# Four seven-product pairs instead of three in each feed-forward layer, the last one split by row blocks at the layer's end

## The reference, cut to what matters

```
D_MODEL, D_FF, SEQ = 1024, 2816, 256

def swiglu(x, w_in, w_out):
    gate, up = jnp.split(x @ w_in, 2, axis=-1)
    return (jax.nn.silu(gate) * up) @ w_out

h = layer_norm(DN_ALPHA * h + 0.5 * swiglu(h, ffn_w_in[i, 0], ffn_w_out[i, 0]), ...)
```

## Time and profile before

| | |
|---|---|
| time, 3 runs | median 1494.35 us (1494.21 to 1494.43) |
| the profiled execution: its own time | 1494.24 us |
| its span in the trace | 1492.2 us |
| PE busy | 1479.8 us, 99% of the span |
| DVE busy | 1112.4 us, 75% |
| ACT busy | 832.2 us, 56% |
| DMA | 310.08 MB, 208 GB/s mean |

### The profile page before, as it was taken

How to read it: one execution, slowest core, us unless ns; L and a number is a source line. 1 busy time by engine, 2 the same in 40 slices (tenths; PEclk the granted TensorE clock), 3 DMA queues, 4 the chain that set the end, 5 groups by cost and what they waited for, 6 DMA issues and landing times.

```text
span 1492.2 us, 18605 instructions
## 1 busy us (share of the span) xinstructions
PE 1479.8 (99%) x7654; PEld 1255.3 (84%) x7654; DVE 1112.4 (75%) x1135; ACT 832.2 (56%) x839; POOL 148.6 (10%) x152
## 2 busy tenths in 40 slices
PE   9999999999999999999999999999999999999997
PEld 8788888888888888888888888888998888888886
DVE  7879677788878888686576788867786566776555
ACT  6656566566656666454434666645555666454443
POOL 0200010200002000034030200002002200020000
PEclk9999999999999999999999999999999999999999
DMA  9884554588558676555544678655444434465551
GB/s 378 294 254 171 219 213 169 198 296 297 169 198 299 219 265 185 217 219 193 176 152 171 269 252 262 190 212 197 170 170 170 141 141 165 148 236 185 197 197 58
DMA packets 46595, 310.08 MB, mean 208 GB/s; under 512 B 5568, under 2 KB 6016, under 8 KB 10800
## 3 DMA queue, kind: packets, MB, share of 16 engines
q1 hardware_dynamic: 38592, 270.35, 48.4%
q0 software_dynamic: 6112, 34.80, 10.1%
q10 hardware_dynamic: 1808, 3.74, 0.6%
HBM read 282.60 MB, written 1.05 MB: 190 GB/s over the span
## 4 chain that ended last, share of the span: by engine, by line
PE 91%; DVE 5%; DMA 2%; ACT 1%; issue 1%; SPq 0%; POOLq 0%; POOL 0%; DVEq 0%
PE psum L2011 16%; PE psum L2015 16%; PE psum L2014 16%; PE psum L2120 8%; PE psum L2147 6%; PE psum L2124 4%; PE psum L2257 4%; PE psum L2261 4%; PE psum L2258 4%; PE psum L2154 3%; DVE weights_lo L1189 3%; PE psum L2043 2%; PE psum L2056 2%; PE psum L2049 2%; DMA weights_raw<-in_weights 1%; DMA weights_raw<-weights_raw 1%
## 5 line engine op out<-in xcount | busy, mean ns | idle before, releaser
L1189 DVE TENSOR_TENSOR weights_lo<-weights_raw,weights_hi 128x2048 fp32r<-128x2048 f32 x191 | 440.5, 2308 | 196.4 <-ACT weights_hi L613 195.1
L613 ACT ACTIVATE weights_hi<-weights_raw 128x2048 fp32r<-128x2048 f32 (+1 forms) x198 | 372.5, 1883 | 202.7 <-PE psum L2015 136.2
L2011 PE MATMUL psum<-weights_hi,hidden_hi 128*128 128x512 f32 x416 | 163.2, 392 | 1.3 <-DVE weights_lo L1189 1.3
L2014 PE MATMUL psum<-weights_lo,hidden_hi 128*128 128x512 f32 x416 | 162.4, 390 | 0.0
L2015 PE MATMUL psum<-weights_hi,hidden_lo 128*128 128x512 f32 x416 | 162.0, 389 | 0.0
L2011 PE MATMUL psum<-weights_hi,operand 128*128 128x512 f32 x384 | 151.5, 394 | 0.0
L1189 DVE TENSOR_TENSOR weights_lo<-weights_raw_more,weights_hi 128x2048 fp32r<-128x2048 f32 x52 | 119.1, 2290 | 41.7 <-ACT weights_hi L613 41.7
L2014 PE MATMUL psum<-weights_lo,operand 128*128 128x512 f32 x384 | 149.8, 390 | 0.0
L2015 PE MATMUL psum<-weights_hi,operand 128*128 128x512 f32 x352 | 137.2, 390 | 0.0
L2120 PE MATMUL psum<-operand,weights_hi 128*128 128x512 f32 x544 | 129.5, 390 | 0.0
L2120 PEld LDWEIGHTS psum<-operand,weights_hi 128*128 128x128 f32 x544 | 100.9, 188 | 20.2
(11 more groups left out here) (395 smaller groups left out, 2802.3 us busy)
## 6 DMA issues: line engine op xcount, KB each, us to landing
weights_raw<-in_weights SPq DMA_DIRECT2D x190, 1024.0 KB, 4.8
weights_raw_more<-in_weights SPq DMA_DIRECT2D x56, 1024.0 KB, 10.6
weights_raw<-weights_raw POOLq DMA_DIRECT2D x8, 1024.0 KB, 9.0
normalised<-in_weights SPq DMA_DIRECT2D x8, 1024.0 KB, 12.8
ln_rows<-in_ln_rows POOLq DMA_DIRECT2D x16, 512.0 KB, 9.3
weights_raw<-weights_raw_more POOLq DMA_DIRECT2D x8, 1024.0 KB, 6.9
weights_raw_more<-weights_raw POOLq DMA_DIRECT2D x4, 1024.0 KB, 13.8
weights_raw_more<-weights_raw_more POOLq DMA_DIRECT2D x4, 1024.0 KB, 12.7
```

The lines of the kernel that those rows point to most:

```text
L613: nc.scalar.activation(hi[:, rest], whole[:, rest], ACT.Copy).then_inc(hi_split, 1)
L1189: nc.vector.tensor_tensor(lo_of(n), raw_of(n), hi_of(n).bitcast(F32), ALU.subtract).then_inc(lo_split, 1)
L2011: mm(out, a_hi, b_hi, start=start, stop=False, skip_group_check=True)
L2014: mm(out, a_hi, b_lo, start=False, stop=False, skip_group_check=True)
```

## The change

`GROUPS` becomes `(3, 5, 7, 9)`: steps 0, 1, 2 plain, and then four pairs one right behind the other, so that the layer ends with the pair of steps 9 and 10. The plain step 5 and the half-wise step 10 are gone. The nine operands of the last pair end with down 8, which is now the first tile of the final `block_product`; so only one down product (of step 7) stands between its sixth and seventh product, and none behind the seventh.

The turning and splitting of the last pair's hidden values goes by token block: `turn_last` of block 0 (4 transposes) inside the down product of step 7, `turn_last` of block 1 inside the final product, behind down 8 of the first token block. ACT and DVE get `last_hidden_hi` and `last_hidden_lo` for one token block each.

The loads of the last pair go only to the five buffers outside the ring (`in_last`). In the first layer POOL issues all t1 and t4 sums ahead of scaling the residual.

```
-GROUPS = (3,6,8,)
+GROUPS = (3, 5, 7, 9)
...
+            in_last += [w and k >= FFN_LOADS.index(("up", GROUPS[-1], 0)) for k, w in enumerate(inside)]
...
+        if in_last[m]:
+            allowed = range(RING, RAW_SLOTS)
...
+            for s in GROUPS[1:]:
+                add_t1(N_FFN0, 0, s)
+                add_t4(N_FFN0, 0, s)
+            load_rows(1)
+            pool.dma_start(cst[:, 1:, :], io["constants"][:, 1:, :]).then_inc(consts_loaded, 16)
             for tb in range(TB):
                 pool.wait_ge(x_loaded[tb], 16)
                 nc.gpsimd.tensor_scalar(resid[:, tb, :], resid[:, tb, :], ALPHA, 0.0, ALU.mult, ALU.add).then_inc(resid_ready, 1)
-            load_rows(1)
-            pool.dma_start(cst[:, 1:, :], io["constants"][:, 1:, :]).then_inc(consts_loaded, 16)
-            for s in GROUPS[1:]:
-                add_t1(N_FFN0, 0, s)
-                add_t4(N_FFN0, 0, s)
...
+                def last_hidden_hi(s, tb):
+
+                    act.wait_ge(group_turned, 2 * group_index(f, s) + tb + 1)
+                    rows = slice(tb * P, (tb + 1) * P)
+                    nc.scalar.activation(hid_hi[:, 0:4, rows], turned_rows(tb), ACT.Copy).then_inc(hid_hi_done, 1)
...
                     split_hi(n + 8)
-                    if s != GROUPS[-1]:
-                        split_hi(n + 9)
+                    if s == GROUPS[-1]:
+                        act.wait_ge(weights_used, n + 7)
+                        last_hidden_hi(s, 0)
+                    split_hi(n + 9)
                     act.wait_ge(weights_used, n + 8)
                     nc.scalar.activation(gate_up[:, 0, :], work[:, 0, 0:TOK], ACT.Silu).then_inc(group_silu, 1)
+                    if s == GROUPS[-1]:
+                        split_hi(n + 10)
+                        last_hidden_hi(s, 1)
...
-                    split_lo(n + 7)
+                    last = s == GROUPS[-1]
+                    if not last:
+                        split_lo(n + 7)
                     dve.wait_ge(group_silu, 3 * g + 1)
-                    nc.vector.tensor_tensor(hid[:, 0:2, :], silu_g[:, :, :], p1_p6[:, :, up], ALU.mult)
+                    first_rows = nc.vector.tensor_tensor(hid[:, 0:2, :], silu_g[:, :, :], p1_p6[:, :, up], ALU.mult)
+                    if last:
+                        first_rows.then_inc(hid_done, 1)
+                        split_lo(n + 7)
                     split_lo(n + 8)
...
+                def turn_last(g, s, tb):
+
+                    pe.wait_ge(hid_done, j0 + s + 1 + tb)
+                    src = hid[:, :, :].rearrange("p c t -> p (c t)")
+                    for c in range(4):
+                        at = (c % 2) * TOK + tb * P
+                        ins = nc.tensor.transpose(work[:, 2 + c // 2, at:at + P], src[:, tb * NCOL + c * P:tb * NCOL + (c + 1) * P], ident)
+                    ins.then_inc(group_turned, 1)
...
-                    next_down(s - 2, n + 6)
+                    last = s == GROUPS[-1]
+                    next_down(s - 2, n + 6, {(1, 0, 1): lambda: turn_last(g, s, 0)} if last else {})
                     pe.wait_ge(combined, 3 * g + 3)
                     product(n + 7, 0, block_of_x(1, 1), False)
-                    next_down(s - 1, n + 8, {(1, 0, 1): lambda: turn_group(g, s)})
+                    if not last:
+                        next_down(s - 1, n + 8, {(1, 0, 1): lambda: turn_group(g, s)})
...
-                        features_halves(n0 + UP_AT[s], pairs, (first_free, second_free), f"ffn{f}", plain_second=True)
...
+                block_product(n0 + FFN_TILES - 3, hid_ready, lambda tb, s: j0 + FFN_STEPS - 2 + (tb + 1 if s else 0),
+                              hidden_chunks((2, 0, 1), 2), final=(1, 3, 4, 6)[f],
+                              hooks={(0, 1, 0, 0): lambda: turn_last(last_group, GROUPS[-1], 1)})
```

More of the change, by code:

```diff
@@ L103 @@
 UP_AT = {s: FFN_OPERANDS.index((("up", s, 0), 1)) for s in ffn_units() if s not in GROUPS}
-WIDE_FROM, WIDE_TO = RING, UP_AT[FFN_STEPS - 1]
+WIDE_FROM, WIDE_TO = RING, FFN_TILES - 3
 def stream_tables():
-    load_of, released, wide_load, wide_operand, in_xn = [], [], [], [], []
+    load_of, released, wide_load, wide_operand, in_xn, in_last = [], [], [], [], [], []
     n = 0
@@ L401, in build @@
         sig_of = lambda half, b: sig[3 if (half, b) == (1, 2) else b]
-        wide = ["ffn0", "gla2", "gla3", "ffn1", "ffn2", "ret1", "ret2", "ret3", "ret4", "ffn3", "sec1", "sec2", "sec8", "sec9"]
+        wide = ["gla2", "gla3", "ret1", "ret2", "ret3", "ret4", "sec1", "sec2", "sec8", "sec9"]
         half_value = lambda what: wide.index(what) + 1
-        copies_of = lambda what: 1 if what.startswith("ffn") else 2
-        copied_value = lambda what, half: sum(copies_of(w) for w in wide[:wide.index(what)]) + half + 1
+        copied_value = lambda what, half: 2 * wide.index(what) + half + 1
         ret_count = lambda u: 6 + u // 2
@@ L764, in ffn @@
                         group(j, n0 + GROUP_AT[j])
[L765 to L771, removed]
+                        second_of_next(after, ahead + 1)
+                        group_hidden_hi(j)
                         if after in GROUPS:
@@ L1317, in hidden_lo, with last_hidden_lo @@
                                             ALU.subtract).then_inc(hid_ready, 1)
[L1319 to L1328, removed]
+                def last_hidden_lo(tb):
+                    dve.wait_ge(hid_hi_done, j0 + FFN_STEPS - 1 + tb)
+                    rows = slice(tb * P, (tb + 1) * P)
+                    nc.vector.tensor_tensor(hid_lo[:, 0:4, rows], turned_rows(tb), hid_hi[:, 0:4, rows].bitcast(F32),
+                                            ALU.subtract).then_inc(hid_ready, 1)
                 def form_sums():
@@ L1411, in group @@
                     nc.vector.tensor_tensor(hid[:, 3, :], gate_up[:, 1, :], p5[:, up], ALU.mult)
-                    if s != GROUPS[-1]:
-                        split_lo(n + 9)
+                    if last:
+                        last_hidden_lo(0)
+                    split_lo(n + 9)
                     dve.wait_ge(group_silu, 3 * g + 3)
-                    nc.vector.tensor_tensor(hid[:, 2, :], gate_up[:, 0, :], work[:, 0, up], ALU.mult).then_inc(hid_done, 2)
+                    nc.vector.tensor_tensor(hid[:, 2, :], gate_up[:, 0, :], work[:, 0, up],
+                                            ALU.mult).then_inc(hid_done, 1 if last else 2)
+                    if last:
+                        split_lo(n + 10)
+                        last_hidden_lo(1)
                 def group_hidden_lo(s):
@@ L1434, in ffn @@
                         group(j, n0 + GROUP_AT[j])
-                        if j == GROUPS[-1]:
-                            split_lo(ahead)
-                            group_hidden_lo(j)
-                            split_lo(ahead + 1)
-                        else:
-                            split_lo(ahead + 1)
-                            group_hidden_lo(j)
+                        split_lo(ahead + 1)
+                        group_hidden_lo(j)
                         if after in GROUPS:
@@ L2320, in ffn @@
                         first_down(n0 + UP_AT[s] + 2, range(2), (0, 1), summed_before(f, 3))
-                    elif s < FFN_STEPS - 1:
+                    else:
                         features_both(n0 + UP_AT[s], unit_banks(s), second_free=second_free)
                         next_down(s - 2, n0 + UP_AT[s] + 2)
-                    else:
-                        features_halves(n0 + UP_AT[s], pairs, (first_free, second_free), f"ffn{f}", plain_second=True)
                     before = s
-                block_product(n0 + FFN_TILES - 3, hid_ready, lambda tb, s: j0 + FFN_STEPS - 2 + s, hidden_chunks((2, 0, 1), 2),
-                              final=(1, 3, 4, 6)[f])
+                last_group = group_index(f, GROUPS[-1])
+                block_product(n0 + FFN_TILES - 3, hid_ready, lambda tb, s: j0 + FFN_STEPS - 2 + (tb + 1 if s else 0),
+                              hidden_chunks((2, 0, 1), 2), final=(1, 3, 4, 6)[f],
+                              hooks={(0, 1, 0, 0): lambda: turn_last(last_group, GROUPS[-1], 1)})
             def warm(count):
```

20 lines of the change are left out of this document (6 added, 14 removed).

## The result

The changed kernel takes 1498.97 us (median of 7 runs, 1497.97 to 1499.90) where the kernel before, on the same chip, takes 1494.11 (7 runs, 1493.98 to 1494.43): a ratio of 1.0034, with an interval from 1.0024 to 1.0043. It is slower by 4.9 us, where 1485.0 was forecast. The profiled execution has a span of 1497.1 us.

The account below looks back on a forecast made before the run. PE was busy 1479.8 of 1492.2 us, so the matmuls themselves were taken as the bound. 1494.24 - 10.0 (matmuls saved) + 0.8 (wait at the layer's end) = 1485.0 us, range 1483.8 to 1491.

Parts of the forecast that it names:

- What PE saves: On PE, dropping steps 5 and 10 for one more pair saves 2.51 us a layer, 10.0 in four layers.
- the 0.8 of the tail: PE's wait for the second turn in the final product: 0.2 us a layer, 0.8 in all.
- No lag behind three pairs: DVE and ACT keep pace through pairs 5, 7 and 9 in a row; no lag builds up: 0.
- t1 of pair 9: Accumulating DMA whose second tile waits for a buffer; lands 22.4 to 24 us into pair 7, costing PE 0.
- L - 26.1: PE's loss in pair 9 if t1 lands L us into pair 7; nothing for an earlier L.
- the nearest row is the 5.7 to 6.9: Duration in us taken for pair 9's t1, from pair 8's t1 landing after a t4 while two loads were under way.
- The bound above, 15.3: Longest duration over all t1, as the other end for pair 9: L 30.8, a loss of 4.7 us a layer.
- The end of the layer: In the final product PE waits for the second turn: 0.2 us a layer, 0.8 in all, from 0 to 0.5.
- The other moves: First layer's x loads and t1, scaling the residual after pair 9's t4, and the next layer's first loads: 0.
- the third: Rival: pair 9's t1 takes 12.9 us or more from issue, making the kernel slower, up to 1504; chance 0.07.
- the rival of the queues that share: Pair 9's t1 and SP's loads take turns in the DMA engines: 5.0 us in all, 1490; chance 0.14.

Follow-up runs that it names:

- e7: Changed kernel with the edits of e3 and e4 together: 1485.24 us, ratio 0.9940 to the kernel before.
- e3: Changed kernel, with b12 of pair 9 allowed a ring buffer that is free earlier, so t1 is issued some 11 us earlier: 1485.81 us.
- e4: Changed kernel, with the first layer's row and constant loads issued after pair 9's t4 lands, which also puts off scaling the residual: 1497.25 us.
- e5: Changed kernel, with b21's load of the last pair waiting on SP for a later low split, about 4 us behind t1's issue: 1485.38 us.
- e9: Changed kernel, with b21's load of the last pair waiting for four dummy POOL operations behind t1's issue: 1485.67 us.

## Why the prediction was wrong

- **What PE saves: right.** Pairs of 30.8, as reckoned. With t1 out of the way and the row loads and the scaling put off, e7 takes 1485.24 us; the sum said 1485.0, or 1484.2 without the 0.8 of the tail, which did not come. PE's last matmul starts 9.25 us earlier than before; 0.36 is lost in the first layer's pair 9 and 0.5 to a late low split of down 10 in the fourth layer, which makes 10.1. That the time comes within 0.3 of 1485.0 is luck: the 0.66 behind the last matmul, which no term had, stands where the 0.8 was put. The count of matmuls was off by 8 turns a layer: 208 fewer in all, not 240; their time was in the sum.
- **No lag behind three pairs: right.** Pairs 5 and 7 have no wait, nor has pair 9 in three layers of e3.
- **t1 of pair 9: the step that failed.** L - 26.1 was right: in the second layer t1 is issued 15.9 into pair 7 and lands at 29.8, which gives 3.7, and 3.74 was lost; in the third and fourth it gives 2.5 and 2.4, and 2.6 was lost in each. What failed is the DMA's own time, "the nearest row is the 5.7 to 6.9, so L is 22.4 to 24, and I take 0". It measured 12.6 to 13.9. The row showed an addition of POOL that was *ahead* of SP's two loads, and I read it as one that runs *beside* two loads without loss. What it really showed was that the loads stood still. For pair 9 the prediction has both numbers, the issue after 15.5 and a load at 15.8, and did not ask which of the two reaches the engines first: the load does, by 0.03 us of issue and 0.47 of start. The bound above, 15.3, was there, and I gave it 7 in 100.
- **The end of the layer: mis-sized.** 0.2 a layer was taken, and no wait of PE on the second turn is in the trace of the changed kernel: 0.
- **The other moves: a second step that failed.** "Scaling the residual now follows the t4 of pair 9 ...: 0" asks only who waits for the scaling, not what runs beside it. It lengthens two of DVE's low splits from 2.28 to 3.13, 1.7 us in the first layer; with the 3.6 of its late t1 that makes 5.3 of the 5.37 lost there. Putting it off in e4 gave 1.7 in the time. The row loads that come right behind that t4 were not named at all; they make it longer (8.0 us, not 6.9), and nothing waits for it.
- **The rivals.** The case that came was the third: t1 at 12.9 us or more from its issue (13.3 in the mean of the four layers). Its mechanism was named as a busier stretch; it was the order of two. The rule of the Trainium skill that I set beside the rival of the queues that share (DMA: Bandwidth & Descriptors, Queues, rings and completion order) says that an engine takes turns between queue rows, but turns of a whole packet, 9 to 17 descriptors as a rule. I had read turns of equal small parts into it. The loads here have 128 packets of 8 KB, 8 for each of the 16 engines if they are spread evenly; if one of these is what the page calls a descriptor, which no run here shows, a whole load would go through in one turn, as the windows show it to do. It does not tell why b22's load then shares with t1 (from 415 to 420 us of the changed kernel both queues have about half). That stays open.

## What to carry to other kernels

When a DMA is tight, ask what reaches the engines just before it, not how many transfers run beside it: one megabyte ahead cost this one 4.9 us, the next, 4 us behind it, 1.5, and the four after that nothing. A row that shows a transfer unharmed beside others shows it only for the order in which they came; look at the packets of each queue in that window to see who waited. When two issues come within 1.5 us, take the worse order as the estimate, or make the order sure, with an earlier buffer (e3, e7) or a wait on the other queue (e5, e9). And of work that a change moves ask not only who waits for it, but what it now runs beside: the scaling on POOL had no one waiting, and cost DVE 1.7 us (e4).

## What the runs showed that I had not expected

- Behind one another, an accumulating DMA of 1 MB takes 6.9 us alone, 11.3 to 12.4 behind one load that reaches the engines 0.5 us before it, 12.6 to 14.5 when a second load follows, and 7.5 to 9.8 when the loads come 1.55 us or more behind it.
- A semaphore that POOL counts up right behind the issue of a DMA lets SP's issue stand 0.07 us behind it, though the issue is shown as 0.84 us long. To be behind it in the engines it had to be later: 1.55 us was enough.
- POOL's one-column product takes 0.23 us (four in 0.92), not the 0.56 that I took from its one-column power.
